# A decoder step on one core: VectorE's attention and sample pieces ahead of the dots in each slot

## What is computed

```python
x = x + concat(diff_attention(q, k, v), pool_mixer(u)) @ w_out    # 4 heads; softmax(q1 k1) - lam * softmax(q2 k2)
xn = rmsnorm(x)
s = einsum('thpd,hpkd->thpk', (xn @ wq).reshape(T, 8, 2, 128), sub_keys)
# top 16 of each half, top 16 of their 256 sums -> 16 experts idx of 16384 for each of 8 heads, gate = softmax(top)
h = gelu(einsum('td,thkd->thk', xn, u_tab[idx]))
x = x + einsum('thk,thkd->td', gate * h, v_tab[idx])
x = x + sigmoid(rmsnorm(x) @ w_gate) * (p @ w_pl)
y = rmsnorm(x)
```

## Time and profile before

| what | us |
|---|---|
| median of 3 runs | 3251.15 (3251.09 to 3255.97) |
| profiled execution | 3252.52 |
| its span, first to last instruction | 3250.5 |
| busy: PE | 2378.8 (73%) |
| busy: VectorE | 2234.0 (69%) |
| busy: POOL | 1326.7 (41%) |
| busy: ACT | 952.1 (29%) |
| bytes moved, 1269 MB | mean 390 GB/s |

### The profile page before, as it was taken

The page is one execution under the profiler, slowest core; times in us unless marked ns, Lnnn a source line. Parts: engine busy times, 40 slices in busy tenths (PEclk is TensorE's granted clock), DMA queues, the critical chain, the costliest instruction groups (busy, mean ns, idle before and its releaser), DMA issues.

```text
span 3250.5 us, 53254 instructions
## 1 busy us (share of the span) xinstructions
PE 2378.8 (73%) x20824; PEld 952.7 (29%) x20824; DVE 2234.0 (69%) x5457; ACT 952.1 (29%) x2428; POOL 1326.7 (41%) x1143
## 2 busy tenths in 40 slices
PE   7779989648877878746876766666777676767666
PEld 3643333213333333312442212122222222222112
DVE  0356676667788788846667666577787777777764
ACT  1212233234344354312322222123332332233222
POOL 0014434333444434425564544344444454444441
PEclk9889999878889989868888887888888798789778
DMA  7559999989999999999999999999999999999994
GB/s 259 173 208 420 421 417 410 415 341 412 410 418 405 406 418 413 416 356 418 416 416 416 416 417 406 406 416 413 407 419 411 420 413 420 412 420 410 420 416 184
DMA packets 211731, 1269.07 MB, mean 390 GB/s; under 512 B 26480, under 2 KB 29832, under 8 KB 70544
## 3 DMA queue, kind: packets, MB, share of 16 engines
q0 software_dynamic: 159808, 1133.76, 85.0%
q1 hardware_dynamic: 50236, 131.61, 10.5%
q10 hardware_dynamic: 1436, 0.29, 0.0%
HBM read 1237.11 MB, written 28.65 MB: 389 GB/s over the span
## 4 chain that ended last, share of the span: by engine, by line
DMA 31%; PE 14%; DVE 7%; issue 2%; POOL 2%; DVEq 2%; ACT 1%; SPq 0%; POOLq 0%; ACTq 0%
DMA ring<-in_uv,idx 29%; PE sc L920 7%; DVE ring L1729 4%; PE sc L953 3%; POOL ring L1910 2%; PE route L895 1%; DVEq L1739 1%; DMA x_scratch<-x 1%; PE sc L922 1%; ACT diag L1287 1%; DMA front<-in_c_band_sp 1%; PE work L941 1%; PE sc L824 0%; ACT hgelu L1282 0%; DVE x L1781 0%
## 5 line engine op out<-in xcount | busy, mean ns | idle before, releaser
L1910 POOL DMA_INDIRECT ring<-in_uv,idx x1056 | 1249.2, 1183 | 1698.2 <-PE sc L922 1428.2
L920 PE MATMUL sc<-ring,diag 32*32 32x512 f32 x8192 | 1239.6, 725 | 695.6 <-ACT diag L1287 646.8
L1729 DVE CUSTOM_DVE_ANT_0 ring<-ring,xn_cur 128x1024 f32<-128x1024 f32 x1056 | 1279.5, 1221 | 633.7 <-DMA ring<-in_uv,idx 628.5
L922 PE MATMUL sc<-ring,diag 32*32 32x512 f32 x8192 | 1239.4, 725 | 0.0
L920 PEld LDWEIGHTS sc<-ring,diag 32*32 32x32 f32 x8192 | 273.1, 118 | 1472.7 <-ACT diag L1287 1024.1
L1282 ACT ACTIVATE hgelu<-hdot 128x2 f32<-128x2 f32 x528 | 107.5, 204 | 1817.1 <-DVE hdot L1729 1810.7
L1287 ACT ACTIVATE diag<-gate_d,hgelu 128x32 f32<-128x32 f32 x1056 | 281.7, 314 | 21.2
L922 PEld LDWEIGHTS sc<-ring,diag 32*32 32x32 f32 x8192 | 272.4, 118 | 1.5 <-issue 1.5
L498 PE MATMUL sc<-big,front 128*128 128x512 f32 x512 | 236.1, 608 | 4.3 <-DVE front L1383 3.6
L1282 ACT ACT_TABLE_LOAD x128 | 164.2, 1283 | 2.2
L895 PE MATMUL route<-big,xnT 128*128 128x256 f32 x560 | 136.7, 399 | 0.0
(11 more groups left out here) (264 smaller groups left out, 2303.6 us busy)
## 6 DMA issues: line engine op xcount, KB each, us to landing
front<-wqk_scratch SPq DMA_DIRECT2D x29, 1024.0 KB
ring<-in_uv,idx POOLq DMA_INDIRECT x1056
big<-in_w_in SPq DMA_DIRECT2D x4, 2048.0 KB, 17.9
wqk_scratch<-front SPq DMA_DIRECT2D x8, 1024.0 KB, 6.6
big<-wqk_scratch SPq DMA_DIRECT2D x8, 1024.0 KB, 18.9
x<-x_scratch SPq DMA_DIRECT2D x13, 512.0 KB
front<-in_x SPq DMA_DIRECT2D x8, 512.0 KB, 8.3
xnT<-in_wq_t POOLq DMA_DIRECT2D x8, 512.0 KB, 3.9
```

The lines of the kernel that those rows point to most:

```text
L920: pe.matmul(sc[own, 0, :], diag[own, r, :], uv_rows[own, r, D:D + W4], start=opens_sum, stop=closes).then_inc(row_added[r], 1)
L922: pe.matmul(sc[other, 1, :], diag[own, r, :], uv_rows[own, r, D + W4:2 * D], start=opens_sum, stop=closes).then_inc(row_added[r], 1)
L1729: dve.tensor_tensor_reduce(uv_rows[:, k % RING, 0:D], uv_rows[:, k % RING, 0:D], xn_cur[:, :], 1.0, 0.0, ALU.mult, ALU.add, hdot[:, n % 2, ...
L1910: pool.indirect_dma_start(uv_rows[:, k % RING, :], None, uv, bass.IndirectOffsetOnAxis(ap=idx[:, n % PH, j:j + 1], axis=0)).then_inc(row_i ...
```

## The change

In VectorE's main loop `front_step(s)` and `sample_step(s)` are called ahead of the two dots and not behind the top-k piece. Nothing else differs: each piece, its slot number and its waits stay, and so do the programs of the other engines. The gate steps stay behind the top-k piece. The slots before slot 0 are not touched.

```diff
--- before.py
+++ after.py
@@ -1859,6 +1859,8 @@
                     open_tile(t)
                 for pair in range(PAIRS):
                     s = n * PAIRS + pair
+                    front_step(s)
+                    sample_step(s)
                     dot(n, 2 * pair)
                     dot(n, 2 * pair + 1)
                     if pair == 0:
@@ -1872,8 +1874,6 @@
                         norm_scale(t + 1)
                     if n + 2 < NN:
                         choose_part(n + 2, pair)
-                    front_step(s)
-                    sample_step(s)
                     for i, (_, s0) in enumerate(GATE_JOBS):
                         gate_step(i, s - s0)
             add_sum(NT)
```

## The result

| | before | after |
|---|---|---|
| median, us | 3251.1 (3251.0 to 3256.0) | 3326.4 (3319.5 to 3328.5) |
| profiled execution, us | 3252.5 | 3319.5 |
| its span, us | 3250.5 | 3317.5 |

The ratio of the medians is 1.0224, with an interval of 1.0206 to 1.0242. The change costs 75 us in the medians and 67 in the profiled runs. The forecast was 3278, so the direction is right and the size is a third of what came. 3326 lies outside the range of 3252 to 3316.

The account below looks back on a forecast made before the run. Transfers were taken to bound the kernel, with VectorE delays costing only when the ring runs dry. 23.1 us from the attention tiles plus 2.5 at slot 70 made 25.6, so 3252.5 + 25.6 = 3278 us, range 3252 to 3316.

Parts of the forecast that it names:

- The bound: Whole kernel: transfers at 405 to 421 GB/s set the pace; VectorE delays cost only when the ring of eight rows empties.
- Part 1, the exponentials: Heads of tiles 2 to 7: `combine` waits 24 times for ACT's exponentials, 2.1 to 3.18 us each.
- Part 2, the scores: Heads: near scores need no wait of size, as VectorE has two pairs of dots between.
- Part 2, the end of a tile: Six tile ends: added waits of 3.8 us at `heads_sum`, 1.0 at `heads_norm`, 2.0 at each `add_out`; 8.8 us a tile.
- Part 3, the sum: Tiles 2 to 7: added waits less spare time, tile by tile, give 39.1 us; after deductions 23.1 us.
- The deductions: Attention tiles: 10.2 us off for old waits swallowed by new ones, and 5.8 us off for the ring.
- The ring's 5.8 us: Row buffer: the full ring hides a VectorE delay of 5.8 us, counted once, at tile 2.
- Part 4 and the rest: Long wait at slot 70 costs 0 to 5.1 us, taken as 2.5; slots 0 to 66 and samples cost nothing.
- A, covered after all: Attention tiles: new waits fall in spare time and the ring hides more than once a tile; 3252 us, chance 0.18.
- B, faster in tiles 2 and 3: Stretch 671 to 749 us: PE's sums and the fetches start sooner, regaining 10 us; 3243 us, chance 0.09.
- C, 3315 us: All six tiles cost, with 3.7 us per `add_out`, 5.1 for slot 70, nothing deducted; 62.2 us more, chance 0.16.
- The signs: Changed trace: reciprocal, squares and `add_out` wait; row waits fall to 20 to 40 us; slots 71 to 192 take 23 longer.

Follow-up runs that it names:

- `combine_behind`: The changed kernel with only the combination put back behind the dots and the top-k piece; 3275.3 us, ratio to before 1.008.
- `exps_first`: The changed kernel with ACT taking the exponentials of tiles 2 to 7 ahead of `weigh` of their slot; 3270.9 us, ratio to before 1.0068.
- `combine_near_behind`: The changed kernel with combination, near scores and largest of tiles 2 to 7 put back behind the dots and top-k piece; 3262.2 us, ratio 1.004.
- `combine_ahead`: The kernel before with only the combination of tiles 2 to 7 moved ahead of the dots; 3279.8 us against 3250.3, ratio 1.0091.
- `near_ahead`: The kernel before with only near scores and largest of tiles 2 to 7 moved ahead of the dots; 3268.1 us, ratio 1.005.
- the delays: The kernel before with 11 added VectorE delays between slots 343 and 503, of 6.7 us each (3270.2 us) or 13.5 us each (3338.9 us).
- `combine_near_heads_behind`: The changed kernel with combination, near scores, largest and `heads_sum` put back behind the dots and top-k piece; 3253.9 us, ratio 1.0012.

## Why the forecast was right in kind and wrong in size

**The bound.** Right. The kernel before runs at the pace of the transfers, and VectorE's delays cost time only when the ring runs dry. The slices and the lost waits for rows show it.

**Part 1, the exponentials.** Right in place, cause and size: 63.4 us forecast, 61.9 measured in 23 waits; 3.18 us a head in tile 7, 3.29 in the head above. By tile it is off by up to 3 us either way (tile 5: 11.0 forecast, 7.9 measured). That they are the main cause is shown from both sides (`combine_behind` 51 us, `exps_first` 55). The switch of the table took 1.28 us again: the load begins at 1322.61 and the exponentials at 1323.91, 1.30 us later. By the Trainium skill's page "ScalarE: Activation LUTs", section "What ACT_TABLE_LOAD costs", a drain stands on top of each; the trace doesn't agree, and leaving it out was right.

**Part 2, the scores.** Wrong. "The scores need no wait of size" counted two pairs of dots between PE's scores and VectorE's piece. It is one: the piece comes one slot after the scores, and PE takes the sums of the slot before ahead of them. What holds PE up shows at the longest of these waits, in tile 2, where VectorE waits 5.29 us until 700.62:

```profile
690.69 1.62 PE L615 MATMUL work<-big,front 128*128 128x128 f32 x6 [7.18 <-ACT front L1125]
...
695.83 3.84 PE L895 MATMUL route<-front,xnT 128*128 128x256 f32 x16
699.60 0.92 PE L584 MATMUL sc<-big,front 64*128 64x384 f32 x4
```

PE stands 7.18 us for ACT's copy of the turned weights, which comes behind the exponentials, and these behind the dots; only then do its sums, the 3.84 us of `route` and the scores follow. The scores wait 12.8 + 7.4 = 20.2 us. Put ahead alone, they and the largest cost 17.8 us.

**Part 2, the end of a tile.** `heads_sum`: 22.8 us forecast (6 x 3.8), 23.4 measured. `heads_norm`: 6.0 forecast, 3.8 measured. `add_out`: 7.8 + 24 forecast, 61.6 measured, the largest miss in a single wait. It is little of the lost time, since these waits cost about 4 us in `combine_near_behind` and put back give nothing at all in the kernel after. `heads_turned` (L1489) had no term and waits 6.9 us.

**Part 3, the sum. This is the step that failed, on waits from Part 2 that were themselves too small.** It took a whole tile as one account and set spare time at its end against waits in its heads. `combine_ahead`, `near_ahead` and the delays show that the two don't meet: time is lost while spare time is left over. Tiles 4 and 5 were forecast below zero; they cost 9.8 and 6.7 us. Tiles 2, 3, 6 and 7 were to cost 9.4, 7.9, 13.6 and 8.2 and cost 14.8, 15.4, 11.1 and 19.3.

The kernel after by itself can't tell the rule from the sizes, since no spare time is left in it. From slot 71 to 193 all of VectorE's waits make 110.5 us before and 189.2 after, 78.7 more, and the stretch is 77.1 us longer. New waits against what stood before, us:

| | exponentials | `add_out` | squares, norm | scores | `heads_turned` | all |
|---|---|---|---|---|---|---|
| forecast | 63.4 | 24.0 | 28.8 | 0 | 0 | 116.2 |
| measured | 61.9 | 53.8 | 26.4 | 17.3 | 6.8 | 166.2 |

Less the 85.7 us of spare time between these slots, that is 80.5 us. So even the forecast's netting, given these waits, would have come near, and 50 us of them were missing. But most of what was missing at `add_out` is spare time under another name. In `combine_near_heads_behind` VectorE waits 43.6 us more at `add_out` than before and 46.0 us less for rows, and the kernel is 3.6 us longer. What a wait costs is therefore read from the kernels in which it is put back. Counted by place they give this:

| waits in the kernel after | us waited | cost when put back |
|---|---|---|
| in the heads: exponentials 61.9, scores 20.2 | 82 | 51 + 13 = 64 |
| at the end of a tile: `add_out` 61.6, `heads_sum` 23.4 | 85 | 8 + 4 = 12 |

Waits in the heads cost 0.78 of their length, waits at the end 0.14. The second row's costs were measured where 84 us of these waits stood, each from the same kernel. So the spare time did pay, but for the second row. The order in which pieces are put back changes the shares: alone, the combination and the scores cost 29.5 + 17.8 = 47.3, together with the rest 64. Alone that is 0.62 of the 47.3 us that the exponentials are waited for and 0.65 of the 27.5 us by which the scores' waits grew. That one ring is emptied by both, while in the single runs each had it for itself, would fit the delay runs; it was not tested. How the shares of single tiles (0.0 to 11.6 in `combine_ahead`) come about wasn't followed slot by slot.

**The deductions.** 10.2 us for old waits swallowed by new ones weren't there: `add_out` waits longer than before, not instead. The ring's 5.8 us, counted once, were near the 5 measured for one delay. How often it hides them in the kernel after isn't shown, as no dot waits for a row there.

**Part 4 and the rest.** Slot 70: 2.5 us forecast. VectorE's wait ahead of the pooled part, in the timeline after:

```profile
664.19 0.69 DVE L1467 TENSOR_TENSOR front<-work,front 128x512 f32<-128x512 f32 x1 [31.96 <-DMA out<-front]
```

It ended at 673.09 before; less the 3.7 us of variation it ends 5.2 us sooner. That is what two rows take (5.1), which fits stores held up by the ring's own bytes; with executions 3 to 4 us apart, one trace doesn't prove it. Slot 71 is 1.0 us later against slot 66 (3.7 - 2.7), which is the cost, at the lower of the two ends that the forecast took the middle of. Slots 0 to 66 and the samples: nothing, as forecast.

**The rivals.** A, covered after all, rests on the same netting and is further off. B, faster in tiles 2 and 3, didn't show: the stretch from 671 to 749 us is at 317 instead of 341 GB/s. C, 3315 us, was nearest, for partly wrong reasons: it made `add_out` dear, which isn't what cost, and its switch of tables took no longer. The forecast's own terms without any netting in the heads, and with the ends of the tiles covered, give 3252.5 + 63.4 + 2.5 = 3318; with 17.3 us for the scores they give 3336. The measured 3326 lies between.

**The signs.** Right: the reciprocal's waits, the squares' 3.9 us a tile, `add_out` above 7.8, the transfers below 405 GB/s, nothing behind the samples. Wrong: the waits for rows were to fall to 20 to 40 us and fell to none, and the stretch of slots 71 to 192 was to grow by 23 us and grew, to slot 193, by 77 (74.4 + 2.7). No version here is faster than the kernel before.

## What to carry to other kernels

Spare time of an engine isn't a sum that pays for waits anywhere in the stage: look for the runs of slots that have none, and charge the waits in them for most of their length (0.6 to 0.8 of it here). Crediting them with 5 us of buffer in every tile was too much. What a buffer hides of one delay can be measured with two delays of known length. Size the waits for an engine by the order of its own queue: count what lies between its work and the piece that waits. And when a wait moves ahead of the work that feeds a bound queue, ask whether the engine waited for has its own input behind that same wait; a wait for an engine that works without a gap anyway only changes its place, and moving it back gains nothing.

## What the runs showed of the hardware

A ring of eight places of 1 MB, with the transfers at 405 to 420 GB/s, hides a delay of 4.9 to 5.4 us of the engine that empties it. At 414 GB/s a row takes 2.5 us, so eight of them are 20 us of transfers, and the ring hides a quarter of that. The trace of the kernel before shows where the other places are. At the dots that waited for a row between 2100 and 3090 us, 4 to 7 fetches had been issued and not yet used, mostly 6, and the row waited for had been issued 9.8 to 21.5 us before (median 14.4). So some two of the eight places are left, and two rows are 5.1 us of transfers. That this is why the ring hides 5 us is an estimate, which no run tested with another number of places. And the loss beyond it is nearly one for one (0.93), though each delay of 13.5 us is followed by 11.4 us of waits for rows (125.2 / 11) before the next.
